# One kernel for two transformer blocks on one core: the loads, the memory's norm, the convolution and a layer norm's sums moved to other places of the program

## The reference, cut to what matters

```
h = concat(meta, x)                                  # 272 tokens
n = rms(h, norm_mix_w);  z = n @ w_in                # q, k, v, glu (2 halves), g_att, g_conv
o = diff_attention(q, k, v)                          # 8 heads, softmax of two maps, difference
y_att = rms(o, subln_w) * (1 - lambda_init)          # norm over each head
u = glu_a * sigmoid(glu_b)
u = causal_dwconv(u, 31 taps) + bias
y_conv = silu(layernorm(u)) @ w_conv_out
h = h + (sigmoid(g_att)*y_att + sigmoid(g_conv)*y_conv) @ w_out
...
memory: k, v = rms(mem, norm_mem_g) @ wkv            # used much later, by the second block
```

## Time and profile before

| | us |
|---|---|
| median of 3 runs | 1295.33 (1295.11 to 1296.21) |
| profiled execution, its time | 1295.04 |
| its span in the trace | 1293.1 |
| TensorE busy | 1190.6 (92%) |
| granted clock, mean | 0.973 |

### The profile page before, as it was taken

How to read it: one execution, slowest core, us unless ns; L and a number is a source line. 1 busy time by engine, 2 the same in 40 slices (tenths; PEclk the granted TensorE clock), 3 DMA queues, 4 the chain that set the end, 5 groups by cost and what they waited for, 6 DMA issues and landing times.

```text
span 1293.1 us, 24300 instructions
## 1 busy us (share of the span) xinstructions
PE 1190.6 (92%) x8716; PEld 1119.8 (87%) x8716; DVE 775.6 (60%) x1318; ACT 572.1 (44%) x1074; POOL 599.2 (46%) x407
## 2 busy tenths in 40 slices
PE   4899999988989999997789999898989989999996
PEld 3899999987879999996788889797869979999996
DVE  4363745679336777746766766666564723666543
ACT  4544444444036565435444545453512634444332
POOL 2666667650035666542443736454201603766641
PEclk9999999988999999998899999999999999999998
DMA  5434344333323445441332323233234515455540
GB/s 234 157 135 148 145 140 152 130 135 130 131 98 131 162 165 189 148 178 70 136 126 93 133 101 126 101 130 130 78 118 163 195 33 195 169 190 187 182 152 33
DMA packets 26008, 179.32 MB, mean 139 GB/s; under 512 B 2784, under 2 KB 3936, under 8 KB 4448
## 3 DMA queue, kind: packets, MB, share of 16 engines
q1 hardware_dynamic: 25520, 176.24, 37.9%
q10 hardware_dynamic: 432, 2.31, 0.4%
HBM read 177.49 MB, written 1.05 MB: 138 GB/s over the span
## 4 chain that ended last, share of the span: by engine, by line
PE 75%; DVE 12%; issue 7%; ACT 4%; DVEq 1%; DMA 1%; POOL 0%; ACTq 0%; SPq 0%
PE ps L527 41%; PE ps L470 11%; PE ps L753 9%; PE ps L818 2%; PE ps L495 2%; ACT parts L997 2%; PE ps L595 2%; DVE work L1678 1%; DVE work L1679 1%; PE ps L567 1%; DVE rinv L1459 1%; DVE parts L404 1%; PE ps L811 1%; PE ps L623 1%; DMA res<-h_in 1%
## 5 line engine op out<-in xcount | busy, mean ns | idle before, releaser
L404 POOL TENSOR_TENSOR parts<-ring,parts 128x1024 fp32r<-128x1024 f32 x184 | 448.4, 2447 | 491.5 <-ACT parts L997 491.5
L527 PE MATMUL ps<-x_high,parts 128*128 128x256 f32 (+2 forms) x3072 | 419.6, 286 | 13.0 <-DVE x_low L1467 4.3
L527 PEld LDWEIGHTS ps<-x_high,parts 128*128 128x128 f32 x3072 | 387.8, 190 | 26.2 <-issue 7.8
L404 DVE TENSOR_TENSOR parts<-ring,parts 128x1024 fp32r<-128x1024 f32 x112 | 258.9, 2313 | 160.4 <-ACT parts L997 160.3
L997 ACT ACTIVATE parts<-ring 128x1024 fp32r<-128x1024 f32 x296 | 295.7, 1049 | 119.9 <-PE ps L753 68.4
L527 PE MATMUL ps<-x_low,parts 128*128 128x256 f32 (+2 forms) x1536 | 217.7, 284 | 0.0
L527 PEld LDWEIGHTS ps<-x_low,parts 128*128 128x128 f32 x1536 | 199.7, 190 | 0.0
L1538 DVE SCALAR_TENSOR_TENSOR ps<-glu,table_sb,ps 128x256 f32<-128x256 f32 x232 | 93.4, 480 | 0.0
L753 PE MATMUL ps<-act_high,parts 128*128 128x256 f32 x704 | 88.4, 283 | 2.6 <-DVE parts L404 2.6
L753 PEld LDWEIGHTS ps<-act_high,parts 128*128 128x128 f32 x704 | 86.2, 191 | 2.8 <-DVE parts L404 2.8
L2001 POOL TENSOR_TENSOR sq<-sq 128x256 f32<-128x256 f32 (+1 forms) x18 | 17.9, 996 | 134.6 <-ACT sq L974 134.6
(11 more groups left out here) (263 smaller groups left out, 1558.0 us busy)
## 6 DMA issues: line engine op xcount, KB each, us to landing
ring<-weights SPq DMA_DIRECT2D x166, 1024.0 KB, 4.7
table_sb<-table ACTq DMA_DIRECT2D x1, 1102.0 KB, 6.0
res<-h_in SPq DMA_DIRECT2D x4, 272.0 KB, 8.6
act<-mem ACTq DMA_DIRECT2D x1, 1024.0 KB, 8.7
out<-xT SPq DMA_DIRECT2D x1, 1024.0 KB, 4.7
work<-positions ACTq DMA_DIRECT2D x1, 128.0 KB, 3.1
```

The costliest lines, as they stand in the source:

```text
L404: eng.tensor_tensor(parts[:, LOW - HIGH + p, cols], ring[:, slot, cols], parts[:, p, cols].bitcast(F32), ALU.subtract)\
L527: mm = pe.matmul(out, left(k), right(k), start=step_ == 0 and k == 0, stop=step_ == 2 and k == KB - 1)
```

## The change

- **Loads.** SyncE waits for `res` and the table before it asks for the first weight chunk; the memory's load goes from ScalarE's queue to SyncE's, behind the fourth chunk.
- **First norm.** VectorE adds the squares of blocks 0 to 6 (6 instructions) and TensorE does 2 matmuls by ones in place of 8. The inverse root goes to a PSUM bank.
- **First pass written out of the loop** on TensorE, ScalarE and VectorE; its chunk 0 is done by `split_chunk` with per-block waits, both tiles at a time, so that it can begin with the first block of the input. ScalarE makes chunk 0's high part ahead of the input's.
- **Memory's norm** in the first pass: squares between the copies of tiles 1 and 2, sum (2 matmuls, bank 7) behind tile 5, root behind the copies of v, norm and low part on VectorE between `combine1(0)` and `maxima1(1)`, high part on ScalarE behind `turned1(0)`.
- **Convolution** of a pair begins in its own pass: `conv_lead` between `maxima1(2)` and `combine1(2)`, 13 of 31 taps in the pass, the rest in the next one or after the last.
- **After the passes.** The layer norm's sums go to bank 3, its squares to `xT`; the sum of the convolution stands before the head sums, and `mem_v(3)`, `mem_v(4)` each stand one place earlier. VectorE scales the convolution before `gate_heads(0)`, and `gate_heads(1)` goes behind three merged tiles of `conv_out`.

```diff
+            sp.wait_ge(res_in, 64)
+            sp.wait_ge(table_in, 16)
             for phase, iters, slots, tiles in PHASES:
                 for c in range(len(slots)):
                     load(phase, 0, c, last[slots[c]])
+                    if phase == "heads1" and c == 3:
+                        sp.dma_start(mem[:, :, :], a["mem"]).then_inc(mem_in, 16)
...
-            norm_sum(T1)
-            norm_sum(SEQ, k_mem)
-
+            norm_sum_of_two(T1, "mix1")
...
+                if start:
+                    split_chunk("heads1", 0, 0, TQ, first=0, x_low=x_low1, first_token=Q0)
+                for t in range(2 * start, 6):
                     proj(t)
+                if start:
+                    norm_sum_of_two(SEQ, "mem", k_mem, 7)
                 pe.wait_ge(kv_ready, n.next(kv_ready))
                 scores1(0)
...
+            pe.wait_ge(conv_ready, 1 + KB)
+            channel_sum(CONV_BANK, conv, TQ, conv_ready)
             mem_v(5)
-            head_sums(lambda j: sq[:, 4 + j, 0:TQ], TQ, squared)
-            channel_sum(4, conv, TQ, conv_ready)
+            att_first = n.before(squared, HEADS)
+            head_sums(lambda j: sq[:, j, 0:TQ], TQ, squared, att_first)
+            pe.wait_ge(centered, KB)
+            channel_sum(CONV_BANK, xT, TQ, squared)
+            n.before(bank_read[CONV_BANK])
             mem_v(6)
+            head_sums(lambda j: sq[:, 4 + j, 0:TQ], TQ, squared, att_first + 4)
             mem_v(7)
-            channel_sum(5, sq, TQ, squared)
-            n.before(bank_read[5])
...
-            sc.dma_start(mem[:, :, :], a["mem"]).then_inc(mem_in, 16)
...
+                if start:
+                    root_of_mean(7, SEQ, D, "eps6", root[:, 0:SEQ], rooted)
+                    sc.wait_ge(consts_ready, 1)
+                    sc.activation(lam_t[:, 2:4], lam_t[:, 0:2], ACT.Exp).then_inc(lb_exp, 1)
                 ahead1(2)
                 exps1(0)
...
                 turned1(0)
+                if start:
+                    x_high_parts(mem_high, k_mem, SEQ, NORMS["mem"] * KB)
                 exps1(1)
...
+            def pair1(i, earlier):
+
+                if earlier is not None:
+                    conv_taps(earlier, 13, 25)
+                maxima1(0)
+                if earlier is not None:
+                    conv_taps(earlier, 25, 27)
+                combine1(0)
+                if earlier is None:
+                    norm(SEQ, lambda k: mem[:, k, :], lambda k: k_mem[:, k, :], "norm_mem_g_2", 2)
+                    x_low_parts(mem_low, k_mem, mem_high, SEQ, "mem")
+                if earlier is not None:
+                    conv_taps(earlier, 27, 29)
+                maxima1(1)
+                if earlier is not None:
+                    conv_taps(earlier, 29, TAPS)
+                combine1(1)
+                glu1(i, 0)
+                glu1(i, 1)
+                maxima1(2)
+                ve.wait_ge(tile_read[STREAM.bank("heads1", 9)], STREAM.before("heads1", i, 9) + 1)
+                conv_lead(i * 2)
+                combine1(2)
+                conv_taps(i * 2, 0, 4)
+                maxima1(3)
+                conv_taps(i * 2, 4, 6)
+                combine1(3)
+                conv_taps(i * 2, 6, 13)
...
-            conv_lead(6)
-            conv_taps(6, 0, 5)
+            conv_taps(6, 13, 18)
             ve.wait_ge(meta_exp, 1)
...
-            conv_taps(6, 5, TAPS)
-
-            ve.wait_ge(bank_full[4], n.next(bank_full[4], 3))
+            conv_taps(6, 18, TAPS)
```

More of the change, by code:

```diff
@@ L595, in products @@
                             mm = pe.matmul(ps[:, banks[e], 0:width], w[:, k * CW + e * P:k * CW + e * P + P],
-                                           x[:, k, 0:width], start=begin and k == 0, stop=end and k == KB - 1)
+                                           x[:, k, first_token:first_token + width], start=begin and k == 0,
+                                           stop=end and k == KB - 1)
                             if end and k == KB - 1:
@@ L1065, in _ @@
                 ahead1(0)
+                if start:
+                    sc.wait_ge(mem_in, 16)
+                    for k in range(KB):
+                        act_fn(k_mem[:, k, :], mem[:, k, :], ACT.Square, squared)
                 for t in (2, 3):
@@ L1454, in step, with norm, add_squares @@
                 ve.wait_ge(dve_step, n.next(dve_step))
-            def norm(width, src, dst, weight, roots):
+            def norm(width, src, dst, weight, roots, inverse=rinv):
                 ve.wait_ge(rooted, roots)
-                step(ve.reciprocal(rinv[:, 0:width], root[:, 0:width]))
+                step(ve.reciprocal(inverse[:, 0:width], root[:, 0:width]))
                 for k in range(KB):
-                    ve.scalar_tensor_tensor(dst(k), src(k), col(weight, k), rinv[:, 0:width], ALU.mult, ALU.mult)\
+                    ve.scalar_tensor_tensor(dst(k), src(k), col(weight, k), inverse[:, 0:width], ALU.mult, ALU.mult)\
                       .then_inc(normed, 1)
+            def add_squares(which, src, width):
+                for k in range(1, KB - 1):
+                    ve.wait_ge(squared, SQUARES[which] * KB + k + 1)
+                    ins = ve.tensor_tensor(src[:, 0, 0:width], src[:, 0, 0:width], src[:, k, 0:width], ALU.add)
+                    if k < KB - 2:
+                        step(ins)
+                    else:
+                        ins.then_inc(summed, 1)
             def x_low_parts(dst, src, high, width, name):
```

135 lines of the change are left out of this document (64 added, 71 removed).

## The result

The changed kernel takes 1282.19 us (median of 4, 1281.38 to 1283.23) against 1295.77 for the kernel before: ratio 0.9894 [0.9879, 0.9909], 13.6 us faster, where 22 were forecast. 1282.19 lies above the stated range of 1267 to 1281. The profiled execution took 1283.23, its span is 1281.4 and its mean granted clock 0.973, the same as before.

What follows compares the result with a forecast made beforehand. TensorE, busy 92% of the span, was taken to bound the kernel. Start -13.1, first pass +5, passes 2 to 4 +1 and end -14.7 sum to -21.8: likeliest 1273 us, 8 in 10 from 1267 to 1281.

Steps and rivals of the forecast that it cites:

- The stretch behind the passes: First v tile to end of `conv_out`: 65.3 us in place of 80.0, a gain of 14.7.
- res lands at about 8.6: Start: the input arrives at about 8.6 us in place of 11.19, bounds 7.5 and 10.
- TensorE starts chunk 0 at 16.6: Start: TensorE's first weight chunk begins at 16.6 us instead of 26.79, behind the first scaled block.
- nothing else is in flight: Start: table and `res`, 2.2 MB, load alone at 426 GB/s, taking 5.2 us with some tail.
- its low part ... 2.9 after GpSimd lets VectorE in at 20.1: Start: the input's low part takes 2.9 us from 20.1; chunk 0 ends at 26.
- The 41.7: End of the start: first attention scores at 41.7 us instead of 54.84, a gain of 13.1.
- I take +5: VectorE mostly first, as at 25.11: First pass, memory's norm before `turn1(1)`: 5 us lost, with VectorE mostly ahead of GpSimd and part of a clock loss.
- the second rival: First pass: GpSimd goes first, stall 7.9 plus clock, 10.5; 1279, or 1282 with the passes' 4; chance 0.25.
- The lower bound: First pass: TensorE waits 3.1 us at `turn1(1)` for the memory's reciprocal, scalings and low parts, without GpSimd going first.
- Passes 2 to 4: +1 forecast: `conv_lead` in unit 2 leaves no slack but little loss: 1 us for all passes, bounds 0 and 4.
- The slower rival: `conv_lead` in unit 2 stops TensorE in each of four passes, some 6 us per pass: 1297, chance 0.03.
- Everything behind conv_out is the same program shifted: Stretch after `conv_out`: unchanged program at an earlier time, difference 0.

Runs made afterwards that it cites:

- The end alone: Only the convolution in its own pass and the moved layer norm sums, against the kernel before; loads and both norms as before: 1282.3 us, ratio 0.99.
- weights at once: Changed kernel, but SyncE asks for weight chunks from the beginning; the memory's load stays behind the fourth chunk: 1281.64 us, ratio 0.9893.
- ScalarE's wait: Changed kernel, but ScalarE converts the second chunk only when the input's low parts are done: 1279.72 us, ratio 0.9868.
- root in PSUM: Changed kernel, but the memory's inverse root is written to a free PSUM bank: 1279.2 us, ratio 0.9859.
- the reciprocal twice: First norm's reciprocal done twice, on the changed kernel: 1278.97 us, ratio 0.9876; on the kernel with the memory's norm spread: 1272.65 us, 0.9814.
- the root in SBUF: Changed kernel, but the first norm's inverse root stays in SBUF, as before the change: 1283.3 us, ratio 0.9902.
- norm spread: Changed kernel, memory's norm split over gaps of the first pass, its root in PSUM: 1271.52 us, ratio 0.9795; again 1268.36 us, 0.9787.

## Why the prediction was wrong, point by point

- **Direction and the end: right.** The stretch behind the passes was to be 65.3 and is 64.9. Its terms: leading tokens' wait gone (yes, the probabilities at 275.1 as forecast), half clock gone (yes), 1.4 for the taps (0.24: the taps ended at 285.3, TensorE reached them at 285.1, later than 284.0), `silu` no wait (0.5 allowed). The end alone gives a ratio of 0.99.
- **"res lands at about 8.6", "TensorE starts chunk 0 at 16.6": 8.98 and 18.44.** The loads were 0.4 late and the additions kept that distance (12.58); the sum's two matmuls, priced at "6.03/8" each, took 2.15 together instead of 1.5, and root, reciprocal and the first high block the rest. For the high block the forecast left 0.1 (16.5 to 16.6); it took 0.6 behind the first scaling. This mis-sized chain is 1.8 of the 3.9 that the start missed. The reason given for the load, "nothing else is in flight", was half wrong: only the memory had to go (weights at once: 9.02).
- **"its low part ... 2.9 after GpSimd lets VectorE in at 20.1", then "both in time": failed.** This is the same contention as in the second norm, and I priced it there and not here. The row took 7.64, TensorE waited 2.00 and, in the changed kernel's profiles, lost 1.5 in the next chunk to half clock. With ScalarE's wait the first scores came 2.3 sooner, of which 1.5 are this clock (44.15 with the same wait at full clock). The 41.7 was out of reach by the chain above.
- **"I take +5: VectorE mostly first, as at 25.11": the step that failed in the first pass.** The likeliest case was the wrong one; the second rival, "GpSimd first", priced stall 7.9 plus clock, 10.5, and 9.6 was measured (6.81 and 2.8). That this rival's 1279 to 1282 comes so near to 1282.19 is luck: it adds 4 for the passes, which was 0, and knows nothing of the 3.9 at the start. The row at 25.11 was a true reading, but GpSimd had been idle there when VectorE's row began, and in the case in hand it was not; what that is worth stands below. The lower bound's plain work (17 instructions in one piece) was right in kind and a little high: with the root in PSUM and one loss left (2.04 in the low part) the stall was still 4.54, so some 2.5 without any, where 3.1 was priced.
- **Passes 2 to 4: +1 forecast, 0.0 measured.** `conv_lead` did stand behind GpSimd (3.71 for two products, priced at 4.43), and `turn1(2)` never waited. The slower rival has nothing for it.
- **"Everything behind conv_out is the same program shifted": off by 3.0 in the profile.** The program is the same; its granted clock was lower, which is at least a part of it. In medians it weighs less: the first four terms sum to -14.7, and the medians differ by 13.6, 14.6 and 13.0 to 13.5 in three comparisons.
- **The size.** -21.8 became -11.7 in the profiles: +3.9 start, +4.6 first pass, -1 passes, -0.4 end, +3.0 behind. Start and first pass failed by the same thing, once not priced and once taken as unlikely: VectorE instructions with two SBUF inputs that stood for whole GpSimd instructions.

**What decides who stands.** The input's low part is eight instructions with two SBUF inputs, and in every profile in which the second chunk is not held back GpSimd's row begins 1.56 to 1.58 us behind its start. In seven profiles it took 2.90 and GpSimd's first two 6.0 (before three times, the end alone, the reciprocal twice in two kernels, the root in SBUF); in seven it took 7.62 to 7.65 and GpSimd's 5.06 (changed three times, root in PSUM, norm spread twice, weights at once). What separates them without exception: in the first seven GpSimd was idle when VectorE's row began, in the other seven its preceding instruction still ran for 0.5 us (16.43 + 4.70 is 21.13, the row begins at 20.61). The memory's scalings at 53.29 began in the same way, 0.2 before GpSimd's row from 48.76 ended, and lost too.

Why that should decide is not shown, and three things in the traces narrow it down. First, the half instruction of overlap costs only 0.4 by itself: in the three profiles with the second chunk held back the row began just so and took 3.28 to 3.29. Second, it isn't where in a VectorE instruction GpSimd's row begins: 0.12 to 0.15 us into one in the rows that lost, 0.09 to 0.22 in those that didn't. Third, a rival fits as well: how long GpSimd had paused. Before the seven long rows it was idle for 1.05, before the memory's scalings for 0.36, and before every row that went through for 2.98 or more (5.83 at the spread norm's low part, over 20 at a later input's low part, between 578 and 604 us of every kernel). No run tells a short pause from a row that begins during GpSimd's work; one that shifts VectorE's row alone by small steps would.

By the Trainium skill ("GPSIMD Engine Reference", section 1) the two share SBUF interfaces when a VectorE instruction has two SBUF inputs; the scalings of 3.23 with the root in PSUM against 7.54, and 6.73 against 3.36, agree. That section doesn't say who stands.

**Open**: what sets the moment at which the clock rises in chunk 0, and with it, as it seems from seven profiles, whether it falls behind the wait of 2.00; and which of the two values (945 or 948) an execution has behind `conv_out`. A median of several executions levels it, a ledger of two profiles does not. No run has the start's edits alone, or the six additions, or chunk 0 by blocks alone: of the 9.2 us by which the first scores came sooner, 2.2 are the load's, and how the rest divides is open.

## What to carry to other kernels

Find each row of VectorE instructions with two SBUF inputs that meets GpSimd, also in stretches that the edit only moves in time, and price each at two whole GpSimd instructions until a trace shows otherwise; put one operand into PSUM, or let the row start while GpSimd is idle (in these traces GpSimd's pause was 2.98 us or more at the rows that went through, 1.05 or less at those that didn't). Work that is moved off the start should be cut to the gaps of its new place: in one piece it cost 9.6 us, in three pieces nothing. A difference of 3 us between two profiles of this kernel in a stretch whose program didn't change is within what one program shows (945.03 and 947.91) and is left out of the causes; one of 1.5 is so at the start.

## What the runs showed of the hardware that I had not expected

- More work need not be slower: with a second reciprocal of 1.86 us the first scores came 2.05 us sooner in the profile, 1.5 of it by the clock. The medians don't show a gain (0.9876 against 0.9886 to 0.9894; on the norm spread 0.9814 against 0.9795).
- A VectorE row beside the same GpSimd row is stretched from 2.90 to 7.64, or left alone. In fourteen profiles it was stretched whenever GpSimd's instruction before still ran for half a microsecond as it began.
- The same 2.00 us of waiting was followed by a granted clock of 0.59 or of 1.00, also for one and the same program (norm spread: first scores at 45.46 with 0.60, at 43.95 with 1.00).
